# Pooling after the first MLP: each group's product made on unnormalised tokens between the MLP's output tiles, the windows as a product with bands

## The reference

```python
def multiscale_pool(h, w_groups, scale):
    B, L, D = h.shape
    hf = h.astype(jnp.float32).reshape(B, L, POOL_GROUPS, POOL_G)
    t = jnp.arange(L, dtype=jnp.float32)
    diffs = []
    for gi, w in enumerate(POOL_WINDOWS):
        c = jnp.pad(jnp.cumsum(hf[:, :, gi], axis=1), ((0, 0), (w, 0), (0, 0)))
        win = c[:, w:] - c[:, :L]
        cnt = jnp.minimum(t + 1.0, float(w))[None, :, None]
        diffs.append(win / cnt - hf[:, :, gi])
    d = jnp.stack(diffs, axis=2).astype(h.dtype)
    y = jnp.einsum('blgc,gce->blge', d, w_groups).reshape(B, L, D)
    return y * scale

def squared_relu_mlp(h, w_up, w_down):
    a = jax.nn.relu(jnp.einsum('bld,df->blf', h, w_up))
    return jnp.einsum('blf,fd->bld', a * a, w_down)

# first block, for layer in range(2):
        u = rmsnorm(h, mix_norm[layer])
        if layer % 2 == 0:
            ...
        else:
            mix = multiscale_pool(u, pool_w[o], pool_scale[o])
        h = h + mix
        h = h + squared_relu_mlp(rmsnorm(h, mlp_norm[layer]), w_mlp_up[layer], w_mlp_down[layer])
```

## Time and profile before

| | us |
|---|---|
| median of 3 runs | 1338.77 (1337.21 to 1340.76) |
| the profiled execution | 1337.13 |
| its span, first to last instruction | 1335.3 |
| PE busy | 1287.9 (96%) |
| DVE busy | 918.2 (69%) |
| ACT busy | 728.6 (55%) |
| mean granted TensorE clock | 0.983 of full |

### The profile page before, as it was taken

The page is one execution under the profiler, slowest core; times in us unless marked ns, Lnnn a source line. Parts: engine busy times, 40 slices in busy tenths (PEclk is TensorE's granted clock), DMA queues, the critical chain, the costliest instruction groups (busy, mean ns, idle before and its releaser), DMA issues.

```text
span 1335.3 us, 24846 instructions
## 1 busy us (share of the span) xinstructions
PE 1287.9 (96%) x10413; PEld 1257.7 (94%) x10413; DVE 918.2 (69%) x1557; ACT 728.6 (55%) x1231; POOL 4.5 (0%) x13
## 2 busy tenths in 40 slices
PE   5998999999999899999999999999999999999997
PEld 5897779999999899999999999999999999999997
DVE  4579636666544866644486599985687757999655
ACT  5745224656333366533455566664676766666544
POOL 1000000000000000000000000000000000000000
PEclk9999969999999899999999999999999999999999
DMA  6232104455555065555375366656355433666640
GB/s 250 87 119 86 58 0 132 142 185 174 174 174 174 18 215 181 188 189 181 121 228 183 111 198 196 190 185 217 104 155 195 127 127 127 192 199 190 210 127 32
DMA packets 58314, 204.98 MB, mean 154 GB/s; under 512 B 6323, under 2 KB 8668, under 8 KB 57948
## 3 DMA queue, kind: packets, MB, share of 16 engines
q1 hardware_dynamic: 56816, 201.77, 46.3%
q10 hardware_dynamic: 1388, 1.64, 0.4%
HBM read 202.32 MB, written 1.06 MB: 152 GB/s over the span
## 4 chain that ended last, share of the span: by engine, by line
PE 84%; DVE 8%; ACT 6%; issue 1%; DMA 1%; ACTq 0%; DVEq 0%
PE PS L351 67%; PE PS L399 7%; PE PS L433 2%; ACT WH L329 2%; PE PS L382 1%; DVE WL L336 1%; PE PS L480 1%; PE PS L2061 1%; ACT EE L2219 1%; PE PS L666 1%; PE PS L362 1%; DVE Z L1431 1%; PE PS L704 0%; ACT L492 0%; PE PS L703 0%
## 5 line engine op out<-in xcount | busy, mean ns | idle before, releaser
L336 DVE TENSOR_TENSOR WL<-RAW,WH 128x1024 fp32r<-128x1024 f32 (+2 forms) x383 | 460.3, 1208 | 233.2 <-ACT WH L329 232.8
L329 ACT ACTIVATE WH<-RAW 128x1024 fp32r<-128x1024 f32 (+2 forms) x383 | 391.6, 1042 | 245.8 <-PE PS L351 220.2
L351 PE MATMUL PS<-UH,WH 128*128 128x256 f32 (+2 forms) x1592 | 453.5, 285 | 7.7 <-DVE UL L1416 3.0
L351 PE MATMUL PS<-UH,WL 128*128 128x256 f32 (+2 forms) x1592 | 453.3, 285 | 0.0
L351 PE MATMUL PS<-UL,WH 128*128 128x256 f32 (+2 forms) x1592 | 453.0, 285 | 0.0
L351 PEld LDWEIGHTS PS<-UH,WH 128*128 128x128 f32 (+1 forms) x1592 | 302.4, 190 | 9.0 <-issue 4.7
L351 PEld LDWEIGHTS PS<-UH,WL 128*128 128x128 f32 (+1 forms) x1592 | 302.6, 190 | 0.0
L351 PEld LDWEIGHTS PS<-UL,WH 128*128 128x128 f32 (+1 forms) x1592 | 301.0, 189 | 0.0
L351 PE MATMUL PS<-HL,WH 128*128 128x272 f32 (+1 forms) x512 | 145.8, 285 | 0.0
L351 PE MATMUL PS<-HH,WH 128*128 128x272 f32 (+1 forms) x512 | 145.6, 284 | 0.0
L351 PE MATMUL PS<-HH,WL 128*128 128x272 f32 (+1 forms) x512 | 145.4, 284 | 0.0
(11 more groups left out here) (360 smaller groups left out, 1953.5 us busy)
## 6 DMA issues: line engine op xcount, KB each, us to landing
RAW<-wpack SPq DMA_DIRECT2D x365, 512.0 KB, 3.6
RAW<-wpack SPq DMA_DIRECT2D x16, 384.0 KB, 3.8
X<-xin SPq DMA_DIRECT2D x1, 1088.0 KB, 5.1
C<-cst SPq DMA_DIRECT2D x1, 1072.0 KB, 10.0
HB<-bias_rows ACTq DMA_DIRECT2D x1, 1024.0 KB, 5.4
out<-X SPq DMA_DIRECT2D x4, 256.0 KB, 2.3
RAW<-wpack SPq DMA_DIRECT2D x2, 256.0 KB, 3.5
PI<-pin ACTq DMA_DIRECT2D x2, 256.0 KB, 3.0
```

Source lines behind the costliest of these rows:

```text
L329: a.e.activation(WH[n % NH][:, 0:w], RAW[n % NR][:, 0:w], ACT.Copy).then_inc(*a.mark("wh", n))
L336: v.e.tensor_tensor(WL[n % NH][:, 0:w], RAW[n % NR][:, 0:w], WH[n % NH][:, 0:w].bitcast(f32), ALU.subtract).then_inc(*v.mark("wl", n))
L351: ins = t.e.matmul(o, part(n, hw, kw, a, b), x(kx), start=first and not i and not p, stop=last and i == len(kcs) - 1 and p == 2)
```

## The change

The factor of the norm and the window both act on tokens, the group's weights on features, so the order is turned. The product of a group with its weights is made first, on X times gain, without the root, and with tokens on the partitions: the stationary operand is a tile of tokens (16, 128 and 128, `TILES`), the moving one the 256 output features (`tensor_group`, 18 products a group). The root of a token is then a factor of its partition, applied by ScalarE (VH, `high`) and VectorE (VL, `low`) in one step with the split. The windows, with average and difference, are a product with a band matrix of constants that brings the result back to features on the partitions (`tensor_pool`, six products for each of eight tiles: two of 256 columns, two of 128, two of 16). The band is exact in fp32r, so only the data has a low part.

Groups 0, 1 and 2 are done inside the output stage of MLP 0, while the next pair of tiles is made, after the fourth of its eight units; ScalarE copies them out of PSUM to VF (`scalar_group`). Half of the sums of squares is made there too. Group 3, the rest of the sums, root, VH and VL and the band products come after the MLP. The spread is gone. The fillers are 8, 8 and 6 instead of 18, 50, 8, 14 and 18. The pooling's weights are four units of 256 KB instead of two of 512 KB. The constants lose an unused 128 x 128 matrix; the bands (512 KB) are loaded by a transfer on ScalarE's queue and copied to fp32r by ScalarE during MLP 0. VectorE's adds of the pooled tiles (`vector_pooled`) move from the end of the pooling into the first loop of MLP 1, two at a time.

```diff
@@ -50,14 +50,15 @@
     proj("hg", "w_in", 0, 1536, 2048)
     proj("wout", "w_out", 0, 0, 1024)
     for layer in range(2):
-        if layer == 1:
-            u.append(("pool", "pool_w", 0, None, 0))
-            u.append(("pool", "pool_w", 0, None, 2))
         proj("up", "w_mlp_up", layer, 0, 4096)
         for g in range(4):
             for kcs in blocks(32):
+                if layer == 0 and g and kcs[0] == 16:
+                    u.append(("pool", "pool_w", (0, g - 1), [0, 1], cols(0, 256)))
                 for c in (256 * g, 256 * g + 128):
                     u.append(("down", "w_mlp_down", layer, kcs, cols(c, c + 128)))
+        if layer == 0:
+            u.append(("pool", "pool_w", (0, 3), [0, 1], cols(0, 256)))
...
+    bw, bw0 = np.zeros((128, 4, 256), np.float32), np.zeros((16, 4, 16), np.float32)
+    for n, w in enumerate((2, 4, 8, 16)):
+        d = np.arange(256)[None, :] - np.arange(128)[:, None]
+        bw[:, n] = ((d >= 0) & (d < w)) / w - (d == 0)
+        d = np.arange(16)[None, :] + 16 - np.arange(16)[:, None]
+        bw0[:, n] = (d < w) / w
...
-            keep_going(t, 18)
+            keep_going(t, 6 if layer else 18)
...
+                    if layer == 0 and gg and k0 == 8:
+                        tensor_group(t, gg - 1)
+                        if gg == 3:
+                            root_begin(t, "pool", 0, T, ("rs", "pool"))
...
+                if layer == 0:
+                    gg = i // 8 - 1
+                    if i == 4:
+                        a.e.dma_start(BWF[:, :], cst[:, CAT["bw"]:CAT["bw"] + 1024]).then_inc(*a.mark_dma("bwf", 0))
+                        a.e.dma_start(BW0F[:, :], cst[0:16, CAT["bw0"]:NC1]).then_inc(*a.mark_dma("bwf", 1))
+                    if i == 7:
+                        a.wait_ge("bwf", 1)
+                        a.e.activation(BW[:, :], BWF[:, :], ACT.Copy)
+                        a.e.activation(BW0[:, :], BW0F[:, :], ACT.Copy).then_inc(*a.mark("bw"))
+                    if gg >= 0 and i % 8 == 1:
+                        scalar_split_pool(a, (2 * gg, 2 * gg + 1))
+                        square(a, "pool", 0, gg, X[:, 2 * gg:2 * gg + 2, :], T)
+                    if gg >= 0 and i % 8 == 5:
+                        scalar_group(a, gg)
+                    if i == 30:
+                        preload(a, ACT.Sqrt)
         def vector_mlp(v, layer):
             st, w = f"mlp{layer}", T - TOK0[layer]
             tok0 = TOK0[layer]
             end_mlp(v, layer)
...
             for p in range(4):
+                for j in (2 * p, 2 * p + 1):
+                    if layer:
+                        vector_pooled(v, j)
                 for j in (2 * p, 2 * p + 1):
                     split_lo(v, (st, j), UL[:, j, 0:w], X_(j, tok0), g(f"mlp{layer}", j), UH[:, j, 0:w])
...
+                        if layer == 0 and gg and (k0, m) == (0, 1):
+                            vector_split_pool(v, (2 * gg - 2, 2 * gg - 1))
+                            add_squares(v, "pool", 0, gg - 1, T)
...
+        def tensor_group(t, g_):
+            n = unit_at["pool", g_]
+            freed = ("vf", g_) if g_ < 3 else ("vl", 3)
+            b, b0 = banks.take(t, ("pv", g_), freed), banks.take(t, ("pv0", g_), freed)
+            for i, (a, z) in enumerate(TILES):
+                o = PS[0:16, b0, 0:256] if i == 0 else PS[:, b, 256 * i - 256:256 * i]
+                ins = products_rows(t, o, [(n, k, 2 * g_ + k) for k in range(2)], 256, lambda k: UH[:, k, a:z],
+                                    lambda k: UL[:, k, a:z], lambda k: ("ul", "pool", k))
+            ins.then_inc(*t.mark("pv", g_))
+            sig.also(("used", n), ("pv", g_))
         def tensor_pool(t):
-            keep_going(t, 18)
-            root_sum(t, "pool", 0, T, ("py", 3, 1))
-            root_spread(t, "pool", T)
-            keep_going(t, 50, "pool")
+            keep_going(t, 8)
+            root_end(t, "pool", 0, T)
+            tensor_group(t, 3)
+            keep_going(t, 8)
+            t.wait_ge("bw")
             for j in range(8):
-                if j in (2, 4):
-                    keep_going(t, (8, 14)[j // 2 - 1], "pool")
-                gi, m = j // 2, j % 2
+                g_, es = j // 2, slice(128 * j, 128 * j + 128)
                 b = banks.take(t, ("pool", j), ("res", "pool", j))
-                k = 2 * (gi % 2)
-                products(t, PS[:, b, 0:S], unit_at["pool", gi // 2], [(k, 2 * gi), (k + 1, 2 * gi + 1)], 128 * m,
-                         128 * m + 128, lambda k: UH[:, k, 0:S], lambda k: UL[:, k, 0:S],
-                         lambda k: ("ul", "pool", k // 2)).then_inc(*t.mark("pool", j))
-            for x in range(2):
-                sig.also(("used", unit_at["pool", x]), ("pool", 4 * x + 3))
+                t.wait_ge("vl", (0, 1, 1, 3)[g_])
+                for p, (v, v0) in enumerate(((VH, VH0), (VL, VL0))):
+                    t.e.matmul(PS[:, b, 0:256], v[:, 0, es], BW[:, 256 * g_:256 * g_ + 256], start=p == 0, stop=False)
+                    t.e.matmul(PS[:, b, 128:256], v[:, 1, es], BW[:, 256 * g_:256 * g_ + 128], start=False, stop=False)
+                    ins = t.e.matmul(PS[:, b, 0:16], v0[:, es], BW0[:, 16 * g_:16 * g_ + 16], start=False, stop=p == 1)
+                ins.then_inc(*t.mark("pool", j))
+        def scalar_split_pool(a, js):
+            for j in js:
+                a.wait_ge("res", "mlp0", j)
+                split_hi(a, ("pool", j), UH[:, j, :], X[:, j, :], g("mix1", j))
+        def scalar_group(a, g_):
+            src = PS[:, banks.at["pv", g_], :].rearrange("p (i e) -> p i e", i=2)
+            a.wait_ge("pv", g_)
+            a.wait_ge("hl", 0, 31)
+            a.e.activation(VF[:, :, 256 * g_:256 * g_ + 256], src, ACT.Copy)
+            a.e.activation(VF0[:, 256 * g_:256 * g_ + 256], PS[0:16, banks.at["pv0", g_], 0:256], ACT.Copy).then_inc(
+                *a.mark("vf", g_))
+        def pool_parts(g0, g1):
+            es = slice(256 * g0, 256 * g1)
+            if g0 < 3:
+                src = [VF0[:, es], VF[:, 0, es], VF[:, 1, es]]
+            else:
+                b = banks.at["pv", 3]
+                src = [PS[0:16, banks.at["pv0", 3], 0:256], PS[:, b, 0:256], PS[:, b, 256:512]]
+            return ((1, src[1], VH[:, 0, es], VL[:, 0, es]), (2, src[2], VH[:, 1, es], VL[:, 1, es]),
+                    (0, src[0], VH0[:, es], VL0[:, es]))
         def scalar_pool(a):
-            for p in range(4):
-                for j in (2 * p, 2 * p + 1):
-                    a.wait_ge("res", "mlp0", j)
-                square(a, "pool", 0, p, X[:, 2 * p:2 * p + 2, :], T)
-            preload(a, ACT.Sqrt)
+            a.wait_ge("acc", "pool", 1)
+            a.free["sq", 1] = ("sum", "pool")
+            for m in range(2):
+                a.wait_ge("res", "mlp0", 6 + m)
+                a.e.activation(SQ[1][:, m, :], X[:, 6 + m, :], ACT.Square).then_inc(*a.mark("sq", "pool", 3, m))
+                scalar_split_pool(a, [6 + m])
             root_sqrt(a, "pool", T)
-            for gi in range(4):
-                a.wait_ge("pd", gi)
+            def high(g0, g1):
+                a.wait_ge("rr", "pool")
                 a.wait_ge("down", 0, 3, 24, 1)
-                a.e.activation(UH[:, 2 * gi:2 * gi + 2, 0:S], Y[:, 2 * gi:2 * gi + 2, NM:T], ACT.Copy).then_inc(
-                    *a.mark("uh", "pool", gi))
-            act_split(a, unit_at["pool", 0] + NH)
+                if g0 == 3:
+                    a.wait_ge("pv", 3)
+                for i, src, vh, _ in pool_parts(g0, g1):
+                    n = 128 if i else 16
+                    a.e.activation(vh, src, ACT.Copy, scale=rooted("pool", i, n)).then_inc(*a.mark("vh", g0, i))
+            high(0, 1)
+            high(1, 3)
+            high(3, 4)
+        def vector_split_pool(v, js):
+            for j in js:
+                split_lo(v, ("pool", j), UL[:, j, :], X[:, j, :], g("mix1", j), UH[:, j, :])
         def vector_pool(v):
-            for p in range(4):
-                add_squares(v, "pool", 0, p, T)
+            vector_split_pool(v, (6, 7))
             root_recip(v, "pool", T)
-            v.wait_ge("down", 0, 3, 24, 1)
...
-            low(3)
-            dve_split(v, unit_at["pool", 0] + NH)
-            for j in range(8):
-                v.wait_ge("pool", j)
-                v.e.scalar_tensor_tensor(out=X_(j), in0=PS[:, banks.at["pool", j], 0:S], scalar=g("psc", j), in1=X_(j),
-                                         op0=ALU.mult, op1=ALU.add).then_inc(*v.mark("res", "pool", j))
+            def low(g0, g1):
+                for i, src, vh, vl in pool_parts(g0, g1):
+                    n = 128 if i else 16
+                    v.wait_ge("vh", g0, i if g0 < 3 or i == 0 else 2)
+                    ins = v.e.scalar_tensor_tensor(out=vl, in0=src, scalar=rooted("pool", i, n), in1=vh.bitcast(f32),
+                                                   op0=ALU.mult, op1=ALU.subtract)
+                ins.then_inc(*v.mark("vl", g0))
```

(35 more changed lines are left out.)

29 lines of the change are left out of this document (14 added, 15 removed).

## The result

The changed kernel takes 1341.28 us, median of 20 runs (1337.34 to 1344.61), against 1337.99 us for the kernel before, run beside it (20 runs, 1334.69 to 1342.05): a ratio of 1.0022, 95% interval 1.0013 to 1.003. By the ratio it is slower by 2.9 us (the medians are 3.3 apart); forecast were 6.4 us less. The difference is small, but with 20 runs of each it is clear of the noise. The profiled execution took 1344.61 us, with a span of 1342.8.

The account below looks back on a forecast made before the run. TensorE bounds the kernel except in the pooling stretch, set by VectorE's chain. 15.40 - 29.04 + 7.22 = -6.42 us, carried over to the 1338.77 us median, gave 1332.3 us; range 1328.0 to 1335.5.

Parts of the forecast that it names:

- The price ahead of the end of MLP 0: First MLP on TensorE: three groups' products and half the sums of squares add 7.22 us.
- No wait inside MLP 0: First MLP: added ScalarE and VectorE work fits idle time; TensorE waiting there for a pooled-input split would disprove the forecast.
- VectorE's chain to 7.86 us: Tail after the first MLP: VectorE is free to start adding pooled tiles at 7.85 us.
- The wait for pooled tile 4's bank and the clock behind it: Before the second MLP: TensorE idles 2.4 us until pool 4's add, then a clock fall loses 1.75 us.
- I take 0.099, since fp32r runs in one pass in all its rows.: Band products in the tail: each narrow product takes 0.099 us, making a block of six 0.63 us.
- rival B: Narrow band products cost 0.235 us, a block 1.11; bank wait hidden, no idle: saving 6.97, 1331.8 us; chance 0.14.
- I expect it at 13.65: Start of the second MLP: clock falls once, after the idle, costing 1.75 us; stretch L = 15.40 us.
- Rival C: Clock falls repeatedly, in band blocks and second-MLP products: L = 18.25, saving 3.6, 1335.2 us; chance 0.09.
- the absent idle: Sign of being wrong: TensorE's idle before the second MLP is absent or over 4 us.
- a narrow product over 0.2 us after the one before it: Sign of being wrong, in the band blocks: narrow products start over 0.2 us apart.
- the ring of banks up to MLP 1: Eight PSUM banks in rotation: followed only to the second MLP's first product, which waits for x plus pool 4.

Follow-up runs that it names:

- experiment 5: Changed kernel with six ring banks skipped before the last four attention output tiles and the head tile made 128 rows high: 1332.61 us, ratio 0.9951.
- experiments 9: Changed kernel with six ring banks skipped before the last four attention output tiles and the head tile 64 rows high: 1336.36 us, ratio 0.9987.
- 10: Changed kernel with six ring banks skipped before the last four attention output tiles and the head tile 32 rows high: 1336.39 us, ratio 0.998.
- experiment 11: Changed kernel with 128-row head tile, six ring banks skipped, and VectorE's pooled-tile adds one step ahead: 1330.28 us, ratio 0.9934.
- experiments 1: Changed kernel with six ring banks skipped before the last four attention output tiles, so later banks match the kernel before: 1337.01 us, ratio 0.9986.
- 2: Kernel before with two ring banks skipped before the last four attention output tiles, nothing else: 1343.62 us, ratio 1.0044.
- experiment 3: Changed kernel with six ring banks skipped and all band products 256 columns wide, bands padded with zeros: 1341.72 us, ratio 1.002.
- grouped (4): Changed kernel with six ring banks skipped and each block's six band products grouped by the tile's rows: 1333.97 us, ratio 0.9964.
- no last fillers (12): Changed kernel with 128-row head tile, six ring banks skipped, pooled adds one step ahead, and no six fillers before MLP 1: 1329.04 us, ratio 0.9927.
- 6: Changed kernel with 128-row head tile and three ring banks skipped before the last four attention output tiles: 1335.54 us, ratio 0.9971.

## Why the prediction was wrong

**Right.** The price ahead of the end of MLP 0: three groups and a pass of sums take 2.12, 2.11, 2.10 and 0.78 = 7.11 us, 7.22 forecast. (That MLP 0 ends 9.19 us later in this trace has another 2.0 us in it, which arose before 75 us in unchanged code: the granted clock from 40 to 75 us was 0.90 there, 0.95 before, and from 0.90 to 1.00 in the profiled runs of one kernel and another.) No wait inside MLP 0. VectorE's chain to 7.86 us. The wait for pooled tile 4's bank and the clock behind it: absent in the changed kernel, since TensorE came later still, but there as soon as the blocks were short (experiment 5).

**The first step that failed: "I take 0.099, since fp32r runs in one pass in all its rows."** I bounded a narrow product by its passes and its columns, and looked up the rows of the stationary tile only as a duration (426 against 431 ns). That row tells what one product takes, not when the next one may start. The pitch depends on the neighbours: between tiles of equal rows the half-block takes 0.34 us (experiment 5), with one change down and one up 0.58, whether 16, 32 or 64 rows (experiments 9, 10). So two changes cost 0.24 us, and the 16 pairs of the eight blocks 3.8 us at full clock.

The Trainium skill (TensorE: Matmul & The Clock Gate, "LDWEIGHTS") counts columns alone; by its figure of 1/1.2 ns a column my estimate for the six loads of a block is 6 x 107 = 642 ns. With equal rows the runs agree (0.68 us); with a change of rows they do not (1.16), and the section has no such term.

By itself the pitch would not have broken the forecast. At a block of 1.16 us and full clock TensorE would have come to MLP 1 about 15 us after the end of MLP 0, with the expected idle hidden, as in rival B, which had 1.11: still a gain.

**The step that failed with it: "I expect it at 13.65", one fall of the clock, behind the idle, for 1.75 us.** The clock fell inside the blocks, where TensorE's records leave no idle, and stayed at its lower level to their end. Ten half-blocks and six fillers took 10.68 us there; at full clock they would take 10 x 0.58 + 0.82 = 6.6 (the 0.82 from experiment 11). So the clock cost 4.1 us in the tail and 1.3 behind it, 5.4 against the 1.75 of the forecast. Rival C had the fall in the blocks, but priced it at 1.1 us on short blocks. That the slow blocks bring the fall is shown by the runs side by side: it came in all six kernels with changes of rows, in none of the five with equal ones. What in them brings it is open.

Of the signs of being wrong the absent idle came, and so did a narrow product over 0.2 us after the one before it: the 128-column ones start 0.22 us behind the 256-column ones (446.37 to 446.59). But with equal rows it is 0.21 us (446.57 to 446.78), so that sign could not tell the two apart; the sum over a half-block does, 0.58 against 0.34.

**The second: a step that isn't there.** I followed the ring of banks up to MLP 1 and no further. It has a memory: whatever is taken shifts all that comes after. The forecast thus had this term at nothing; experiments 1 and 2 price it at about 5 us (4.8 to 5.9).

**The sum, set right.** Take the tail, add what the first 72 products of MLP 1 took beyond the 8.58 us of the earlier trace rows, add the 7.11, subtract 29.04. For the change as it is: 19.10 + 1.31 + 7.11 - 29.04 = -1.52, and with 5 us for the ring +3.5; measured +2.9 (+1.7 to +4.0; the ratio and its interval times the median of before). The same sum for the versions with the ring put back:

| kernel | tail | 72 products | sum | measured, 95% interval |
|---|---|---|---|---|
| ring back (1) | 19.14 | 9.85 | -1.5 | -1.9 (-3.7 to 0.0) |
| 256 columns (3) | 23.80 | 9.37 | +2.7 | +2.7 (+1.3 to +4.1) |
| grouped (4) | 16.71 | 9.47 | -4.3 | -4.8 (-6.4 to -3.1) |
| 128 rows (5) | 14.64 | 10.26 | -5.6 | -6.6 (-9.1 to -4.0) |
| 64 rows (9) | 19.66 | 9.69 | -1.2 | -1.7 (-3.6 to +0.3) |
| 32 rows (10) | 17.75 | 10.11 | -2.6 | -2.7 (-4.4 to -0.9) |
| adds ahead (11) | 12.61 | 8.48 | -9.4 | -8.8 (-11.3 to -6.4) |
| no last fillers (12) | 11.79 | 8.70 | -10.0 | -9.8 (-12.1 to -7.5) |

The measured value of all eight lies within 1.0 us of the sum, and the sum within each interval: one stretch accounts for the time of each. The forecast of 1332.3 us is what experiment 5 gave (1332.61): it priced a change with equal rows and an unmoved ring. That the two agree to 0.3 us is partly luck: the tail there was 14.64 us for 13.65, the idle 2.03 for 2.4, the loss to the clock 1.68 for 1.75, and by the ratio the saving is 6.6 us (4.0 to 9.1).

## What to carry to other kernels

When products of different contraction heights are mixed, look at the starts of neighbouring products, not at the duration of one; pad the short tile to full height, or at least put the products of one height together. When an edit changes how many buffers are taken from a ring, follow the ring to the end of the program, wherever fixed and rotating buffers meet, before giving the change a price. And an idle removed is only worth something if what comes behind it isn't waiting for the same engine.

## What the runs showed of the hardware

- Changing the number of rows between successive stationary tiles costs time. One change down and one up cost 0.24 us together at full clock where the short tile's product has 16 columns (0.58 against 0.34 us a half-block), the same for 16, 32 and 64 against 128 rows, and 0.38 us where all products have 256 columns (0.74 against 0.36, experiment 3). At half clock the half-block with 16 columns takes 0.93 us.
- Products of 128 moving columns in fp32r can start 0.06 us after the one before them; over a stream of 256, 128 and 16 columns the mean is 0.34 / 3 = 0.113 us.
- In all six kernels whose blocks change rows the clock fell to its lower level (1.2 GHz; 0.50 and 0.51 of full in the windows) within the blocks: 3.1 to 3.5 us into them in five of the six, 5.9 us with 32 rows, by the chain of waits. In none of the five with 128 rows did it fall in the blocks. Whether the pauses between products or the rows that stand empty do it is left open.
- An idle of 2.03 us ahead of MLP 1 was followed by a lower clock both times it occurred (experiments 5 and 6: 10.26 and 10.24 us for 72 products); one of 1.36 us ahead of the same products, in the kernel before with a shifted ring, was not (8.74 us, granted clock 1.00).
